# Moving VectorE instructions at three places of a two-block transformer kernel

## The reference, cut to what matters

```
mod = jnp.split(sc @ w_mod[l] + b_mod[l], 6, axis=-1)        # modulation rows
p = xn @ w_in[l]                                             # 512 + 256 tokens
y = conv_general_dilated(glu, dw_w, padding 15, one filter per channel, 31 taps) + dw_b
y = silu(layer_norm(y, ln_g, ln_b)); conv = y @ w_pw
mix = concatenate([attn, four, conv, pool]) @ w_o
x = x + gate1 * mix
xn = rms_norm(x, g2) * (1 + scale2) + shift2
x = x + gate2 * swiglu(xn, w_fi, w_fo)                       # (silu(a) * g) @ w_fo
```

## Time and profile before

| | |
|---|---|
| runs | 2222.93, 2229.55, 2230.54 us; median 2229.55 |
| the profiled execution | 2225.05 us, of which span 2223.0 |
| TensorE busy | 2142.9 us, 96% of the span |
| VectorE busy | 1286.6 us, 58% |
| ScalarE busy | 829.0 us, 37% |
| GpSimd busy | 622.1 us, 28% |
| DMA | 219.57 MB, mean 99 GB/s |
| mean granted TensorE clock | 0.985 of full speed |

### The profile page before, as it was taken

One profiled execution on the slowest core, in us unless ns is written; L12 is line 12 of the kernel. 1 busy time (PEld: TensorE's weight loads), 2 busy tenths in 40 slices (PEclk: granted clock), 3 DMA queues, 4 the chain that ended last, 5 costly groups with the idle time before them and its releaser, 6 DMA issues.

```text
span 2223.0 us, 27642 instructions
## 1 busy us (share of the span) xinstructions
PE 2142.9 (96%) x10866; PEld 1767.1 (79%) x10866; DVE 1286.6 (58%) x1869; ACT 829.0 (37%) x1345; POOL 622.1 (28%) x324
## 2 busy tenths in 40 slices
PE   8998899999999999989999999999999999999998
PEld 6884588989999998765778888878788888788656
DVE  6987577777787777797755522254132444532272
ACT  4333425524244253424442222233272222334552
POOL 0000003232222222100244444443234444323402
PEclk9999999999999999999999999999999999989999
DMA  8312241242332424213324232334223333312401
GB/s 324 111 55 83 77 138 53 62 138 86 114 114 84 135 71 132 99 46 123 115 91 159 84 106 88 105 93 142 76 67 95 95 95 97 93 54 57 135 2 57
DMA packets 68497, 219.57 MB, mean 99 GB/s; under 512 B 8208, under 2 KB 13072, under 8 KB 67216
## 3 DMA queue, kind: packets, MB, share of 16 engines
q1 hardware_dynamic: 65920, 212.08, 29.7%
q10 hardware_dynamic: 2448, 5.72, 0.8%
HBM read 210.17 MB, written 2.10 MB: 95 GB/s over the span
## 4 chain that ended last, share of the span: by engine, by line
PE 86%; DVE 7%; ACT 3%; issue 2%; POOL 1%; DMA 0%; POOLq 0%; DVEq 0%; ACTq 0%
PE prod L806 59%; PE prod L871 7%; PE misc L871 5%; PE misc L890 2%; PE prod L973 1%; PE prod L1053 1%; DVE conv_acc L2393 1%; PE prod L1108 1%; PE prod L1021 1%; PE misc L1282 1%; PE misc L960 1%; PE prod L937 1%; POOL wlo L782 1%; PE misc L1132 1%; DVE stat L2324 1%
## 5 line engine op out<-in xcount | busy, mean ns | idle before, releaser
L782 POOL TENSOR_TENSOR wlo<-ring,whi 128x1024 fp32r<-128x1024 f32 (+4 forms) x244 | 504.6, 2068 | 1315.9 <-ACT whi L1370 1315.8
L806 PE MATMUL prod<-operand_hi,whi 128*128 128x512 f32 (+1 forms) x1440 | 518.2, 381 | 11.7 <-POOL operand_lo L755 5.1
L806 PE MATMUL prod<-operand_lo,whi 128*128 128x512 f32 (+1 forms) x1440 | 510.6, 375 | 0.0
L806 PE MATMUL prod<-operand_hi,wlo 128*128 128x512 f32 (+1 forms) x1440 | 510.4, 375 | 0.0
L1370 ACT ACTIVATE whi<-ring 128x1024 fp32r<-128x1024 f32 (+4 forms) x270 | 251.6, 932 | 514.4 <-PE prod L806 486.5
L806 PEld LDWEIGHTS prod<-operand_hi,whi 128*128 128x128 f32 x1440 | 258.4, 189 | 71.0 <-POOL operand_lo L755 7.5
L806 PEld LDWEIGHTS prod<-operand_hi,wlo 128*128 128x128 f32 x1440 | 258.2, 188 | 50.0
L806 PEld LDWEIGHTS prod<-operand_lo,whi 128*128 128x128 f32 x1440 | 258.4, 189 | 47.6
L806 PE MATMUL prod<-hidden_hi,whi 128*128 128x512 f32 (+1 forms) x528 | 188.3, 357 | 2.3 <-DVE hidden_lo L2201 0.9
L806 PE MATMUL prod<-hidden_lo,whi 128*128 128x512 f32 (+1 forms) x528 | 187.9, 356 | 0.0
L806 PE MATMUL prod<-hidden_hi,wlo 128*128 128x512 f32 (+1 forms) x528 | 186.7, 354 | 0.0
(11 more groups left out here) (378 smaller groups left out, 3581.5 us busy)
## 6 DMA issues: line engine op xcount, KB each, us to landing
ring<-in_w SPq DMA_DIRECT2D x224, 512.0 KB, 3.6
modw<-in_wmod SPq DMA_DIRECT2D x68, 512.0 KB, 3.7
ring<-in_w SPq DMA_DIRECT2D x32, 384.0 KB, 3.6
ring<-in_w SPq DMA_DIRECT2D x32, 320.0 KB, 3.0
mod_pair<-in_wpair SPq DMA_DIRECT2D x8, 1024.0 KB, 17.1
ring<-in_wmod SPq DMA_DIRECT2D x12, 512.0 KB, 4.1
dft<-in_dftx SPq DMA_DIRECT2D x8, 512.0 KB, 5.1
resid<-in_xt SPq DMA_DIRECT2D x4, 768.0 KB, 7.2
```

The source lines that it names most:

```text
L782: nc.gpsimd.tensor_tensor(wlo_of(j)[:, 0:w], ring[PLACE["panel", j] % RING][:, 0:w], whi_of(j)[:, 0:w].bitcast(F32), ALU.subtract).then_in ...
L806: mm = pe.matmul(G[b][:, t0:t0 + tn], w[:, k * P:(k + 1) * P], a[:, t0:t0 + tn], start=(i == 0 and q == 0), stop=(i == g.kc - 1 and q == 2))
```

## The change

Only VectorE's order changes. No instruction is added or taken away.

The first edit is at the output product: between two modulation blocks the low part of panel p + 2 is written, where it stood behind both. This holds for the panels 0, 1 and 2, which have two blocks each. The second is in the mixers: beside pair 3 all eight remaining taps are done (54 to 62) in place of four, and the modulation block that stood behind pair 3 goes to pair 4, where the last four taps were. The third is in unit 0: the weight sums for unit 1 follow the first two partial sums in place of going ahead of them.

```
-                    if more:
+                    if more and u:
                         weight_sums(q, u + 1)
                     product_sum(1, 4, 1, P1t[u % 2], P1t[u % 2], b)
                     mod_half(q, u, 0)
                     product_sum(2, 2, 3, C22t, U4t, c)
+                    if more and u == 0:
+                        weight_sums(q, u + 1)
                     if more:
                         sum_low(q, i + 8)
                         sum_low(q, i + 9)
...
                     if l == 0 and i < 5:
-                        conv_taps((52, 52, 54, 58, 62)[i])
+                        conv_taps((52, 52, 54, 62, 62)[i])
+                    if l == 0 and i == 4:
+                        ring_mod(MOD_PE + 6)
 
                 def behind(i, l=l):
-                    if l == 0 and 2 <= i <= 8:
+                    if l == 0 and 2 <= i <= 8 and i != 3:
                         ring_mod(MOD_PE + 3 + i)
...
                 def beside_wout(p, g=GEMM[f"wout{l}"]):
-                    for k in ((1, 2), (3, 4), (5, 6), (7,), (8,), (9,), (10, 11), ())[p]:
-                        own_mod(MOD_RING + k)
+                    blocks = ((1, 2), (3, 4), (5, 6), (7,), (8,), (9,), (10, 11), ())[p]
+                    if blocks:
+                        own_mod(MOD_RING + blocks[0])
                     if p < 6:
                         panel_low(g.j0 + p + 2)
+                    for k in blocks[1:]:
+                        own_mod(MOD_RING + k)
```

## The result

The changed kernel took 2211.77 us, the median of ten runs (2206.53 to 2216.25), against 2225.19 us for ten runs of the kernel before (2217.30 to 2230.54). The ratio is 0.9937, its 95% interval [0.9927, 0.9947]: faster by 0.63%, or 13.4 us between the medians. Five further runs beside the kernel before on one chip gave 2210.86 us and 0.9931 [0.9918, 0.9945]. The forecast was 2213 us, 14.0 us by the profiled execution.

A forecast was written before the change was run, and what follows sets the result against it. TensorE's chain was taken to bound the kernel for 86% of the span. Taps 5.7, low part 3.9 and sums 4.4 make 14.0 us: 2211.0 from the profiled execution, 2215.5 from the median; forecast 2213, range 2205 to 2223.

The forecast's parts named there:

- the three stops: TensorE's waits: 3.56 us for the last taps, 2.13 for panel 2's low part, 3.27 for `value_late` in unit 0.
- Taps: Mixers, pair 4: the 3.56 us wait goes and the ones product regains 2.16 us of half clock; 5.7 us.
- My bound of 3.6: Lower bound of the taps' gain in the mixers: the wait goes but the clock stays low.
- Low part: Output product, panel 2: 2.13 us of waiting and 1.8 of half clock go; 3.9 us, bounds 2.1 to 3.9.
- Panel 3: Output product: its low part would cost 1.0 us behind both blocks; moved too, it ends 1.5 us early.
- The sums: Unit 0: 3.0 us of wait plus 1.6 of half clock, less 0.2 before unit 1's product 1; 4.4 us.
- the low parts of unit 1: Feed-forward unit 1: they were to come 1 us or more before they are needed.
- The clock's share in unit 0: Product 6 takes 3.72 us where twelve such matmuls take 2.08; its half clock costs 1.64 us.
- more than the stops: Rival: the shift also frees the stretch 226 to 237 from half clock, up to 5 us more, 2208; chance 0.08.
- The rival in which this stretch falls to half: Slower: clock at half throughout 217 to 283 adds up to 28 us, 14 us slower, 2241; chance 0.04.
- the clock doesn't come back: Rival at all three stops: only waits go, 8.5 us; 2216.5 by the profiled execution, 2218.5 on the forecast's scale; chance 0.15.
- The rule that I weighed: The gate's time base runs freely of the kernel; by it the sum's 5.5 us of clock would be left out.

The follow-up runs named there:

- second execution: Second profiled execution of the changed kernel, without further edit, level with the kernel before ahead of the first moved place; 2208.01 us.
- first execution: First profiled execution of the changed kernel, 3.4 us late before anything the change moves; 2216.25 us, the slowest of its ten.
- The kernel with the needless matmuls: The kernel before, with four needless `matmul` calls (eight in the profile) on TensorE while it waits ahead of panel 2; 2222.70 us, ratio 0.9987.

## Why the prediction was right, and where not

The forecast was right, and its mechanism held at all three places: the three stops went, and no other signal took their place there. The forecast of the gain was 14.0 us, and 13.4 were measured. Step by step, from the second execution:

- **Taps: 5.7 forecast, 5.74 measured** (5.88 - 0.14), the wait and the clock both. In the first execution it was 4.1 (0.69 + 3.37): the wait went and only 0.4 of the 2.16 us of clock. Five profiled executions of other kernels with all eight taps beside pair 3 also had 2.95 us there, so of seven one lost the clock's share. The five that kept the stop took 4.97 to 5.53 us. My bound of 3.6 was for this.
- **Low part: 3.9 forecast, 3.77 measured** (11.01 - 7.24), in both executions. The kernel with the needless matmuls shows the clock's part by itself, 1.6 us, in the one execution profiled. Panel 3 was hidden, as worked out, and would have been late without its own move.
- **The panels' pace: not in the sum.** Four panels at 8.48 in place of 8.32 cost 0.64 us (11.01 to 10.37).
- **The sums: 4.4 forecast, 2.56 measured** (12.95 - 10.39). This is the term that was mis-sized. Unit 0 itself did what was worked out, 14.80 - 10.39 = 4.41: the restart gave 3.0 us, and product 6 with the wait of about 0.1 us behind it (I had allowed 0.2) the rest. But unit 1 gave back 1.85 us (14.80 to 12.95). The step that failed is that the sum ends with product 1 and the low parts of unit 1. The low parts did come in time, the nearer by 1.7 us, but I had looked at the readers of the moved sums only, and put at nothing, without a reason, what the next unit's own sums do, which stayed in front of `first_product`. VectorE now reaches them later in TensorE's unit: the second sum starts 405.01 - 396.17 = 8.84 us behind the unit's start, where it was 418.33 - 411.14 = 7.19. The moved sums fill that time, and GpSimd's low parts then slow two sums in place of one. `first_product` is 2.6 us later in the unit, 1.65 by the late start and 1.0 by the one more slowed sum. That took the cover. The edit alone shows the wait, moving one more unit's sums moves it on, and moving all ends it. Which of the two shares alone would have been hidden no run shows.
- **The clock's share in unit 0 is the least sure of the three.** Product 6 ran at the full clock in all six profiled executions without the stop, but also in two of the six with it. In those two no clock was lost that an edit could give back.
- **The stretch 217 to 283** gained 1.4 us (5.88 to 7.24), its clock being 0.95 for 0.92; 1.3 in the first execution. That is a small piece of the rival "more than the stops". The rival in which this stretch falls to half did not occur in any profiled run.
- **Behind 428 us the change moves nothing,** yet the second execution gains 4.1 us more (17.03 - 12.95) and the first 0.3. The steps are at norms and attention pieces, where TensorE has idle time and its clock changes: 2.6 us at the norm behind the feed-forward part alone.

So the sum was 14.0, what the three places gave was 5.74 + 3.77 + 2.56 = 12.1 in the second execution and 4.1 + 3.8 + 2.6 = 10.4 in the first, and the rest is the clock elsewhere. That the total landed on 13.4 is in part luck: a missed loss of 1.9 us and small gains of clock nearly cancel. The rival "the clock doesn't come back" (2216.5) describes the first execution's taps and its time, 2216.25, but in that execution the clock did come back at panel 2 and in unit 0, and it began 3.4 us late, so the near match of the time is chance. The rule that I weighed, of the Trainium skill, "TensorE: Matmul & The Clock Gate", Part 1 (not to fit to a specific count of slow matmuls), was half right here: the clock's share was there in most executions, and those where it was not could not be told beforehand.

**Still open.** Why the panels' pace is 8.48 us in ten of twelve profiled executions and 8.32 in two (before, and the sums alone). Both of these have TensorE stop 2.1 us ahead of panel 2, but so do the kernel with only the taps' edit and the one with the taps but not the block moved, which run at 8.48. One difference is on record: in the first two the clock was at half already when TensorE went on (first pair of matmuls 1.01 us), in the other two it fell later (0.62 and 0.61 us). That is a coincidence of four executions, and no run was made to test it.

## What to carry to other kernels

Read a stop of the bounding engine twice, once for its idle time and once for the clock of what follows it, and treat the first as sure and the second as likely. When an edit cures one round of a loop, look for the same order in the rounds left alone: they were covered only by when they ran. Check a gain in the trace by the shift of a common instruction, stage by stage, since the median mixes it with clock changes far behind.

## What the runs showed of the hardware

TensorE's float32 panels of 1024 columns ran at one of two steady paces at the same granted clock, 8.32 and 8.48 us. A VectorE sum with both inputs in SBUF took 0.69 us alone and 1.67 to 1.78 beside GpSimd low parts, while in the trace of before one with a PSUM input kept its 0.54 beside a low part. One program's ones product took 4.64 us in one execution and 2.95 in another. Behind the wait ahead of panel 2 the granted clock was 0.50; with eight needless matmuls inside that wait it was 1.00, in one execution. Behind the unchanged stop of 3.27 us in unit 0 the clock fell in four of six profiled executions: a stop is often followed by the half clock, and not always.
